# Differential heads' norm from one column per token block, and a map scaled by ScalarE, in a two-block transformer kernel on one Trainium2 core

## The reference

```python
sc = einsum('bhcqd,bhckd->bhcqk', qb, k) * scale - slopes * dist     # two maps, c = 0 and 1
p = softmax(where(pos[None, :] <= tq[:, None], sc, NEG_INF), axis=-1)
a = p[:, :, 0] - lam * p[:, :, 1]
diff_out = einsum('bhqk,bhkd->bhqd', a, v)                           # v is 128 wide
diff_out = rms_norm(diff_out, diff_norm_g) * (1.0 - lam_init)        # mean over the head's 128 values
x = x + einsum('bse,ed->bsd', concat([fox_out, diff_out]), w_out)    # 512 + 512 rows of w_out
```

## Time and profile before

| | us |
|---|---|
| median of three runs | 1425.7 |
| the profiled execution | 1427.8 |
| its span, first to last instruction | 1426.0 |
| PE busy / DVE busy / ACT busy | 1375.6 / 990.7 / 707.6 |
| mean granted PE clock, share of full | 0.987 |
| the differential heads, from PE's first transposes of head 0 to PE's first matmul of the second half of the output product | 970.5 to 1034.4 |

### The profile page before, as it was taken

The page is one execution under the profiler, slowest core; times in us unless marked ns, Lnnn a source line. Parts: engine busy times, 40 slices in busy tenths (PEclk is TensorE's granted clock), DMA queues, the critical chain, the costliest instruction groups (busy, mean ns, idle before and its releaser), DMA issues.

```text
span 1426.0 us, 19665 instructions
## 1 busy us (share of the span) xinstructions
PE 1375.6 (96%) x7800; PEld 1186.1 (83%) x7800; DVE 990.7 (69%) x1379; ACT 707.6 (50%) x1145; POOL 127.9 (9%) x103
## 2 busy tenths in 40 slices
PE   8999999999999999999999999999689999999996
PEld 6888888787679999988876888887578999998885
DVE  5799897786677878785228535657777787877332
ACT  4466886633465555562234334454445555555221
POOL 2187335000000000000002000000000000000000
PEclk9999999999999999999999999999899999999998
DMA  9423112477302233416321322110030323233321
GB/s 366 144 87 98 40 41 89 147 219 281 121 16 89 94 115 100 151 60 209 118 89 43 91 88 74 45 31 30 6 142 17 118 92 117 97 126 97 96 89 60
DMA packets 41131, 147.28 MB, mean 103 GB/s; under 512 B 4560, under 2 KB 4816, under 8 KB 40912
## 3 DMA queue, kind: packets, MB, share of 16 engines
q1 hardware_dynamic: 40896, 143.93, 30.2%
q10 hardware_dynamic: 144, 2.10, 0.4%
HBM read 143.91 MB, written 2.10 MB: 102 GB/s over the span
## 4 chain that ended last, share of the span: by engine, by line
PE 85%; DVE 8%; ACT 3%; DMA 2%; issue 1%; SPq 0%; POOL 0%; DVEq 0%; ACTq 0%; POOLq 0%
PE ps L1476 27%; PE ps L1478 27%; PE ps L1477 27%; PE ps L1599 1%; DMA raw<-in_wo 1%; PE ps L1836 1%; DVE t_buf L943 1%; DVE w_lo L895 1%; DVE t_buf L929 1%; PE ps L1823 1%; DMA ada<-in_ada 1%; DVE x L938 1%; ACT w_hi L442 1%; PE ps L1510 0%; PE ps L1544 0%
## 5 line engine op out<-in xcount | busy, mean ns | idle before, releaser
L1476 PE MATMUL ps<-h_hi,w_hi 128*128 128x256 f32 (+1 forms) x1160 | 391.8, 338 | 6.7 <-DVE w_lo L895 3.6
L1478 PE MATMUL ps<-h_hi,w_lo 128*128 128x256 f32 (+1 forms) x1160 | 388.4, 335 | 0.0
L1477 PE MATMUL ps<-h_lo,w_hi 128*128 128x256 f32 (+1 forms) x1160 | 388.2, 335 | 0.0
L895 DVE TENSOR_TENSOR w_lo<-raw,w_hi 128x1024 fp32r<-128x1024 f32 x141 | 183.6, 1304 | 119.7 <-ACT w_hi L442 119.1
L1476 PEld LDWEIGHTS ps<-h_hi,w_hi 128*128 128x128 f32 x1160 | 221.0, 191 | 34.6 <-issue 6.6
L1478 PEld LDWEIGHTS ps<-h_hi,w_lo 128*128 128x128 f32 x1160 | 221.0, 191 | 22.3
L1477 PEld LDWEIGHTS ps<-h_lo,w_hi 128*128 128x128 f32 x1160 | 221.3, 191 | 21.2 <-issue 0.5
L442 ACT ACTIVATE w_hi<-raw 128x1024 fp32r<-128x1024 f32 x141 | 148.4, 1054 | 153.6 <-PE ps L1478 84.7
L885 DVE TENSOR_TENSOR w_lo<-quads,w_hi 128x1024 fp32r<-128x1024 f32 (+1 forms) x152 | 164.9, 1086 | 72.6 <-ACT w_hi L442 72.6
L442 ACT ACTIVATE w_hi<-quads 128x1024 fp32r<-128x1024 f32 (+1 forms) x152 | 144.3, 949 | 78.2 <-PE ps L1478 76.6
L1476 PE MATMUL ps<-act_hi,w_hi 128*128 128x512 f32 x352 | 137.0, 389 | 0.0
(11 more groups left out here) (266 smaller groups left out, 2190.4 us busy)
## 6 DMA issues: line engine op xcount, KB each, us to landing
quads<-in_ffn_in SPq DMA_DIRECT2D x76, 512.0 KB, 4.4
raw<-in_ffn_out SPq DMA_DIRECT2D x44, 512.0 KB, 3.8
raw<-in_ada SPq DMA_DIRECT2D x32, 512.0 KB, 4.3
raw<-in_qk SPq DMA_DIRECT2D x25, 512.0 KB, 3.7
ada<-in_ada SPq DMA_DIRECT2D x16, 512.0 KB, 9.3
raw<-in_gates SPq DMA_DIRECT2D x16, 512.0 KB, 3.7
raw<-in_v SPq DMA_DIRECT2D x12, 512.0 KB, 3.6
raw<-in_ffn_in SPq DMA_DIRECT2D x12, 512.0 KB, 3.7
```

Of the source, the lines that this page charges most:

```text
L895: nc.vector.tensor_tensor(w_lo[p % RING][:], raw[q % RAW][:], w_hi[p % RING][:].bitcast(f32), ALU.subtract).then_inc(raw_used, 1)
L1476: nc.tensor.matmul(out, w[0], v[0], start=start, stop=False, **kw)
L1477: nc.tensor.matmul(out, w[0], v[1], start=False, stop=False, **kw)
L1478: return nc.tensor.matmul(out, w[1], v[0], start=False, stop=stop, **kw)
```

## The change

- The mean of a head is made per token block with the squares as the stationary operand and one column of the 1/128 tile as the moving one: four f32 matmuls of one column (128x128 by 128x1) in place of one of 512 columns. A token then sits on a partition, and the mean is a tile of 128x4.
- DVE's four guard steps, ACT's root and DVE's first product run on 128x4 tiles (`down`, `root_down`, `limit`, `root_d`).
- A new DVE step, `diagonals`, multiplies the identity with each of the four root columns into a tile `diag` of 128x512, and a new PE step, `root_row`, multiplies a tile of 1/1024 with it in one f32 matmul of 512 columns, into bank 3 (bank 6 for the last head). That brings the root back to every partition. `normalise_head` reads it from PSUM, times 1024.
- `combine` is divided: `inverses` makes the three small tiles, ACT scales the second map (`scale_second`, four pieces), and DVE keeps the four additions.
- The lists are written in another order, as shown below the diff. `transpose_map` of heads 2 and 3 waits for the normalised result of head 0 and 1, since they share bank 3.

```diff
             def root_head(h):
                 act.wait_ge(dn_eps, h + 1)
-                link(nc.scalar.activation(rstd[:], rstd[:], ACT.Ln))
-                nc.scalar.activation(rstd[:], rstd[:], ACT.Exp, scale=-0.5).then_inc(dn_rstd, 1)
+                link(nc.scalar.activation(root_d[:], root_d[:], ACT.Ln))
+                nc.scalar.activation(root_d[:], root_d[:], ACT.Exp, scale=-0.5).then_inc(dn_rstd, 1)
+            def scale_second(h):
+                n = HEADS + 2 * h + 1
+                act.wait_ge(inverse, 2 * h + 2)
+                for qb in range(NB):
+                    part = prob_of(n)[:, Q_AT[qb]:Q_AT[qb] + P * (qb + 1)]
+                    nc.scalar.activation(part, part, ACT.Copy, scale=stat[:, n % 4, 2, qb:qb + 1]).then_inc(scaled, 1)
...
             exps(HEADS + 2)
+            scale_second(0)
             prepare("wout_a", 1)
             exps(HEADS + 3)
             for h in range(DH):
                 transposed(HEADS + h)
+                if h + 1 < DH:
+                    scale_second(h + 1)
+                if h:
+                    root_head(h - 1)
                 if h < 2:
                     exps(HEADS + 2 * h + 4)
-                if h:
-                    root_head(h - 1)
...
             def mean_head(h):
-                mean = ps[:, 6, :]
+                mean = ps[:, 6, 0:NB]
...
+            def diagonals(h):
+                dve.wait_ge(dn_rstd, h + 1)
+                link(nc.vector.tensor_tensor(root_d[:], root_d[:], limit[:], ALU.mult))
+                if h:
+                    dve.wait_ge(dn_row, h)
+                for b in range(NB):
+                    nc.vector.tensor_scalar(diag[:, P * b:P * (b + 1)], ident[:], root_d[:, b:b + 1], None, ALU.mult)\
+                        .then_inc(dn_diag, 1)
             def normalise_head(h):
-                dve.wait_ge(dn_rstd, h + 1)
-                link(nc.vector.tensor_tensor(rstd[:], rstd[:], acc[:], ALU.mult))
-                nc.vector.tensor_tensor(o_diff[:, h, :], o_diff[:, h, :], rstd[:], ALU.mult).then_inc(dn_norm, 1)
+                dve.wait_ge(dn_row, h + 1)
+                nc.vector.scalar_tensor_tensor(out=o_diff[:, h, :], in0=o_diff[:, h, :], scalar=float(D),
+                                               in1=ps[:, ROW_BANK[h], :], op0=ALU.mult, op1=ALU.mult).then_inc(dn_norm, 1)
...
             for h in range(DH):
+                if h + 1 < DH:
+                    inverses(h + 1)
                 low(HEADS + h)
+                if h == 2:
+                    combine(h + 1)
+                fox_part((2, 4, 6, 7)[h])
                 if h:
                     mean_head(h - 1)
-                fox_part((2, 4, 6, 7)[h])
                 if h < 2:
                     maxima(HEADS + 2 * h + 4)
                 if h:
+                    diagonals(h - 1)
+                if h < 2:
+                    combine(h + 1)
+                    feed("wout_a", h + 2)
+                clamp_head(h)
+                if h:
                     normalise_head(h - 1)
-                if h + 1 < DH:
-                    combine(h + 1)
                 if h < 2:
-                    feed("wout_a", h + 2)
                     fox_part((3, 5)[h])
                     maxima(HEADS + 2 * h + 5)
-                clamp_head(h)
                 if h:
                     lo_head(h - 1)
             mean_head(DH - 1)
+            diagonals(DH - 1)
             normalise_head(DH - 1)
             lo_head(DH - 1)
...
             def mean_square(i):
                 pe.wait_ge(dn_sq, i + 1)
-                nc.tensor.matmul(ps[:, 6, :], ones_v[:], sq[i % 2][:], start=True, stop=True).then_inc(dn_ms, 1)
+                for b in range(NB):
+                    ins = nc.tensor.matmul(ps[:, 6, b:b + 1], sq[i % 2][:, P * b:P * (b + 1)], ones_v[:, 0:1],
+                                           start=True, stop=True)
+                ins.then_inc(dn_ms, 1)
+            def root_row(i):
+                pe.wait_ge(dn_diag, NB * (i + 1))
+                pe.wait_ge(pt_ready, HEADS + min(i + 2, DH))
+                nc.tensor.matmul(ps[:, ROW_BANK[i], :], ones_d[:], diag[:], start=True, stop=True).then_inc(dn_row, 1)
...
             for i in range(DH):
+                if i >= 2:
+                    pe.wait_ge(dn_norm, i - 1)
                 transpose_map(HEADS + i, prob_of(HEADS + 2 * i))
+                fox_part((2, 4, 6, 7)[i])
                 if i:
                     mean_square(i - 1)
-                fox_part((2, 4, 6, 7)[i])
                 if i < 2:
                     diff_scores(HEADS + 2 * i + 4)
+                if i:
+                    root_row(i - 1)
                 diff_out(i)
...
             mean_square(DH - 1)
+            root_row(DH - 1)
```

More of the change, by code:

```diff
@@ L109, in build @@
         o_diff = place("o_diff", [P, DH, SEQ], f32, at=h_at + 20 * K)
-        down = place("down", [P, SEQ], f32, at=h_at + 28 * K)
-        root_down = place("root_down", [P, SEQ], f32, at=h_at + 30 * K)
+        diag = place("diag", [P, SEQ], f32, at=h_at + 28 * K)
         raw = [place(f"raw{i}", [P, PANEL], f32) for i in range(RAW)]
@@ L131, in build @@
         stat = place("stat", [P, 4, 3, NB], f32)
+        down, root_down, limit, root_d = (place(n, [P, NB], f32) for n in ("down", "root_down", "limit", "root_d"))
         t_at = top[0]
@@ L1325, in qk3_lo, with inverses @@
                 qk_lo_tile("qk3", i, 7, K3_AT[i], i // 4, m_hi, m_lo, i + 1)
+            def inverses(h):
+                n = HEADS + 2 * h
+                sa, sb = stat[:, n % 4], stat[:, (n + 1) % 4]
+                dve.wait_ge(s_exp, NB * (n + 2))
+                link(nc.vector.reciprocal(sb[:, 2, :], sb[:, 1, :]))
+                nc.vector.reciprocal(sa[:, 2, :], sa[:, 1, :]).then_inc(inverse, 1)
+                nc.vector.tensor_scalar(sb[:, 2, :], sb[:, 2, :], lam_s[:, 5:6], None, ALU.mult).then_inc(inverse, 1)
             def combine(h):
@@ L1329, in combine @@
                 first, second = prob_of(n), prob_of(n + 1)
-                sa, sb = stat[:, n % 4], stat[:, (n + 1) % 4]
-                dve.wait_ge(s_exp, NB * (n + 2))
-                nc.vector.reciprocal(sa[:, 2, :], sa[:, 1, :]).then_inc(inverse, 1)
-                nc.vector.reciprocal(sb[:, 2, :], sb[:, 1, :]).then_inc(inverse, 1)
                 dve.wait_ge(inverse, 2 * h + 2)
-                link(nc.vector.tensor_scalar(sb[:, 2, :], sb[:, 2, :], lam_s[:, 5:6], None, ALU.mult))
-                for qb in range(NB):
-                    a, b = Q_AT[qb], Q_AT[qb] + P * (qb + 1)
-                    nc.vector.tensor_scalar(second[:, a:b], second[:, a:b], sb[:, 2, qb:qb + 1], None, ALU.mult)\
-                        .then_inc(scaled, 1)
                 for qb in range(NB):
```

9 lines of the change are left out of this document (6 added, 3 removed).

## The result

The changed kernel takes 1437.6 us (median of four runs, 1435.7 to 1439.4), the kernel before 1425.2 in four runs beside it: a ratio of 1.0083, 95% interval 1.0066 to 1.0100. It is slower by 12.5 us. Forecast were 1434.9 us and a range of 1428.5 to 1441.0. The profiled execution of the changed kernel took 1439.4 us, its span is 1437.5 us.

What follows compares the result with a forecast made beforehand. PE held 85% of the chain of waits, so only its pauses counted. Terms 1.1 + 5.85 + 2.2 gave +9.2 us: 1437.0 against the profiled 1427.8, with the median 2.1 lower, 1434.9; range 1428.5 to 1441.

Steps and rivals of the forecast that it cites:

- N: Time from a head's mean in PSUM to finished diagonals: 2.3 us, bounds 1.9 and 3.1.
- heads 0 and 1, to the transposes of head 2: First heads' passes: gain 3.5 us, loss about 2.95, later about 0.35; net about -0.3 us.
- to the transposes of head 3: Head 3's transposes, waiting for head 1's normalising product, start at 1023.5 against 1022.38: +1.1 us.
- from there to the 96 matmuls, without the clock: Head 3's transposes to the output matmuls: -1.4, +1.4, +1.15, +1.2, +0.05 and +3.45, sum 5.85 us.
- The one-column mean: Four f32 matmuls of one column per head on PE: 1.2 us against 1.15 before, nothing gained.
- a length that cost no clock: Before the first root_row PE pauses 1.8 us, claimed to leave the clock high, so the matmul takes 1.15 us.
- the gain of 3.5 us at 986: With `fox_part(4)` ahead of the first mean, the pause of 2.08 us and about 1.4 us of low clock go.
- The clock term: Low clock after three close pauses of 2.3 to 3.05 us late in the stage: taken as 2.2 us.
- Head 2's pass: PE pauses over 5 us, second root_row from 1015.9 at low clock, head 3's transposes at 1023.5: +1.1 us.
- The clock stays low throughout: Rival: all PE work from 1015 to the first twelve of the 96 matmuls at half rate; +13, 1439 us; chance 0.20.
- Only the last wait costs: Rival: waits in passes of heads 2 and 3 are covered, leaving +3.5 us, 1429; chance 0.10.
- Faster, by DVE's relief: Rival: DVE's backlog is what PE waits for, relief about 2.9 us per head; -4, 1421.7 us; chance 0.07.

Runs made afterwards that it cites:

- e6_guard_ahead: Changed kernel with head 1's guard steps and diagonals ahead of the combination of head 3's maps on DVE: 1435.1 us.
- e5_fill: Changed kernel with idle matmuls that nobody reads in PE's pauses ahead of the four root_row products and the last mean: 1430.2 us.
- e4_mean_later: Kernel before with the forget heads' piece ahead of the mean on PE and ahead of the guard steps on DVE, wide norm kept: 1428.7 us.
- e7_lists: Changed kernel's arithmetic with other lists and banks, each root_row behind PE work that needs nothing of it: 1414.2 us.
- e11_wide_own_lists: Wide norm of the kernel before with ACT scaling, in lists reordered to suit that norm: 1422.1 us, ratio 0.9974 to the kernel before.
- e1_last_row_later: Changed kernel with the last head's root_row moved behind the first twelve of the 96 matmuls on PE: 1434.1 us.
- e2_act_scales_only: Kernel before with only the early small inverses and ACT scaling the second map, norm still wide: 1422.1 us.
- e3_dve_scales: Changed kernel with DVE scaling the second map again, in four pieces inside the combination: 1438.3 us.

## Why the prediction was right, and where it was not

The sign and the kind of cause were right, and the time lies in the range: PE now waits for DVE's diagonals ahead of every `root_row`. The size came out at 12.5 us where 9.2 were forecast, and single steps were off both ways. Here they are, the first two rows of places counted from the first transposes in both kernels (the second contains the first), and the 96 matmuls taken to start where the matmul ahead of them ends in the chain (1034.97 and 1045.36):

| step of the prediction | forecast | measured |
|---|---|---|
| N, mean in PSUM to finished diagonals | 2.3 | 2.3 (pauses of 2.30 and 2.29) |
| pauses before the four root_rows | 1.8, over 5, 2.3, 2.3 | 1.76, 5.71, 2.30, 2.29 |
| wait for the last squares | 3.05 | 3.02 |
| heads 0 and 1, to the transposes of head 2 | -0.3 | +2.05 |
| to the transposes of head 3 | +1.1 | +1.9 |
| from there to the 96 matmuls, without the clock | +5.85 | +8.4 with the clock |
| from there to the sum | 0 | +1.6 |
| clock | +2.2 | in the three rows above |
| sum | +9.2 | +11.9 |

**The durations and the pauses.** N's parts came out near the rows that I took for them. The four guard steps run from 1015.83 to 1016.44, 0.6 us for 0.65; the root takes two times 0.20; the small product and the diagonals together take 1.08 (1042.15 to 1043.23) for 1.1. ACT's scaling takes 1.94 us for four pieces, for 1.9, and is in no chain. The order on DVE gave the pause of over 5 us, and e6_guard_ahead takes 1.85 us of its 5.71 away by moving the maps of head 3.

**The one-column mean.** It takes 0.95 us at the high level, for 1.2. Row 8's loads of 187 ns or more overlap with the matmuls and don't add up, as I had let them. The rule of the Trainium skill (TensorE: Matmul & The Clock Gate, section LDWEIGHTS), 107 ns a load of 128 columns and so an estimate of 0.85 us for eight, was nearer. At the low level the same mean takes 1.86 us.

**The step that failed: "a length that cost no clock".** I let the first `root_row` wait 1.8 us and run at the high level, because a pause of 1.86 us at 1033.82 had been followed by it. It took 2.08 us. Half of what follows ran at 1.2 GHz (0.76 granted from 994.9 to 1006.9), and the transposes of head 2 came 2.05 us later than before instead of 0.3 us earlier. In e5_fill, where the same wait of the same length is filled, they come 0.7 us earlier than before. So the working of the step was right but for the clock, which cost 2.7 us there. e4_mean_later adds that of the gain of 3.5 us at 986, which I set against it, the list edit alone gives 1.3 beside the wide norm.

**The clock term was mis-sized.** From head 3's transposes to the sum it is 2.6 + 1.6 = 4.2 us where I had 2.2. The places are the transposes at 1024.33 (2.14 for 1.31), the last mean (1.86 for 0.95), the last `root_row` (2.08 for 1.12) and the first matmuls of the 96, which follow each other at 0.43 us instead of 0.23 until 1048.7. With head 0's 2.7 the clock comes to about 7 beyond what the steps held, and the filled pauses gave back 6.0. (The low clock of head 2's pass, some 1.4 us, I had in the +1.1.) Even so it was not the last word, since e7_lists is another 19 us of stage shorter than e5_fill. The windows from head 1's transposes to the sum tell the clock from the waits, in this order for the kernel before, the changed kernel, e7_lists and e11_wide_own_lists:

```profile
985.30:1060.90 75.60, 58.53 (x260) 45.55 (x259) 58.88 (x106) 31.49 (x65) 0.00 (x0) 0.90 0.20 69
```

```profile
985.30:1072.90 87.60, 65.82 (x292) 52.27 (x291) 48.83 (x113) 31.86 (x73) 0.00 (x0) 0.84 0.17 60
```

```profile
986.60:1048.70 62.10, 55.96 (x291) 45.52 (x290) 48.33 (x113) 31.74 (x73) 0.00 (x0) 0.99 0.25 85
```

```profile
985.40:1056.70 71.30, 58.14 (x260) 45.30 (x259) 55.62 (x97) 35.11 (x73) 0.00 (x0) 0.93 0.21 73
```

PE's busy time for the same instructions is 65.8 us in the changed kernel and 56.0 in e7_lists: some 9.9 us of the 25.5 between the two windows are the low clock. The other 15.6 are idle time of PE, 21.8 us against 6.1 (17.1 in the kernel before).

**Head 2's pass.** The second `root_row` started at 1018.08, not at 1015.9, because the transposes of head 2 were 2.3 us late; between the two lie 11.2 us, forecast 11.4. From there to the transposes of head 3 it took 6.25 us where I had 7.6: PE went back to the high level within `diff_out(2)`, which I had put at the low one throughout. So the two errors of the clock cancel in part.

**The rivals.** *The clock stays low throughout* is half true: from 1039.1 to 1048.7 it is 0.51, but from 1029.87 to 1036 the high level came back. Its 1439 is nearer to the measured 1437.6 than the forecast's 1434.9. The Trainium skill (the same page, section "What's actually happening") calls the low level the default that activity lifts, and the idle matmuls of e5_fill, which compute nothing and keep the clock up, agree with it. *Only the last wait costs* falls by e1_last_row_later, which gives back 3.1 of 11.9. *Faster, by DVE's relief* falls as a forecast for this kernel, but its mechanism is real: in e7_lists, where nothing waits for N, PE stands idle 6.1 us where it stands idle 13.2 with the wide norm of e11_wide_own_lists, and the time is 7.8 us shorter. By the terms that I named the relief per head is 2.2 us, not 2.9; the 2.9 needs the wide product of 0.69 as well, which also goes. Measured are 10.0 us of DVE's busy time for four heads. I had taken the lists as given and not asked what the same arithmetic would do in others.

## What to carry to other kernels

When a step is made cheaper by a detour over another engine, the busy times say little. Put in the list of the engine that must not stop, behind the detour's start, as much independent work as the detour takes. Here new lists, with the banks that they need, made 1437.6 us into 1414.2. Read a pause of the matrix engine together with the durations behind it: the same matmul at twice its time is part of the pause's price. A single pause that was free in a trace is no proof that another one of its length will be, nor even that the same one will be in the next kernel.

## What was not expected of the hardware

The length of the pause just before does not tell whether TensorE's clock falls. The shortest pause here that was followed by work at the low level (1.2 GHz) is 0.99 us (e4_mean_later, 994.80: granted clock 0.69 from there to 1000). In the same trace 2.92 us were followed by the high level (2.4 GHz) up to the next pause (1030.35). In the changed kernel 1.76 us was followed by the low level (994.95) and 2.30 us by the high one (1033.12). A pause of 2.08 us ahead of the first mean was followed by the high level in e2_act_scales_only (988.10) and by the low one in the kernel before.

One pause shows three outcomes. Ahead of the last mean of the wide norm PE stands idle 1.86 us in the kernel before, 1.87 in e4_mean_later and 1.86 in e2_act_scales_only, ended by the same squares each time. In the first the mean takes 1.13 us and the granted clock is 1.00 from 1034.4 to 1043; in the second the mean takes 1.13, too, but the matmuls from 1035.85 on run at the low level for 3 us; in the third the level falls within the mean (1.62). So a matmul at full speed right behind a pause does not yet show that the pause was free. In the same way the mean behind 3.02 us took 1.86 us in the changed kernel and 1.26 us in e3_dve_scales.

The executions of one kernel differ in their clock, too: in e11_wide_own_lists the fastest, 1416.9 us, has a mean granted clock of 0.993 and the slowest, 1426.0 us, one of 0.985. What decides it besides the pause these runs don't show. A fill of four idle matmuls was enough once (e5_fill, 992.16), and not enough another time (1035.38).
